# Row sums of the first tile on quarters of the PE array, and a fourth context slab held

## Chip, core and metric

The kernel runs on one core of one Trainium2 chip. The metric is device time in microseconds of that core. The engines are PE (TensorE, matrix products), DVE (VectorE), ACT (ScalarE), POOL (GpSimd) and SP (SyncE, which here only issues DMAs). PEld is the weight load of PE, which overlaps its matmuls.

## The reference

Two transformer blocks on 256 tokens of 1024 features, all in float32. The change touches the end of the first block (a mixture of single-neuron experts, "PEER") and the part of the second block that runs beside it (a feed-forward on a separate context of 256 tokens, and the same feed-forward on the 128 tokens of tile 0).

```python
def peer_ffn(h, ...):                # for each block of 128 tokens
    ... 8 heads x 16 chosen experts = 128 expert rows a token
    u_sel = peer_u[expert]
    a = gelu(einsum('bqhkd,bqd->bqhk', u_sel, hb))
    v_sel = peer_v[expert]
    return einsum('bqhk,bqhkd->bqd', g * a, v_sel)
x = x + gate2 * peer_ffn(...)
# second block, with x and with ctx
swiglu(h, w13, w2): a, b = split(h @ w13); (silu(a) * b) @ w2
```

## The kernel before

**Work around the change.** The 256 tokens are two tiles of 128. For each tile the kernel gathers 128 "slots": one indirect DMA by POOL (line 1387) brings, for each of the 128 tokens, the 2048 floats of one expert (u and v side by side), a row tile of 128x2048 float32. Eight buffers hold such row tiles (`GBUF = 8`). Two slots make a batch; tile 0 is batches 0 to 63 (the gather's first half), tile 1 is batches 64 to 127 (the second half).

**For every slot** DVE multiplies u by h and sums (line 2506, `dot_batch`), ACT turns the sum into a weight (lines 1900 and 1831), and then v is added with that weight. In tile 0, PE adds it: ACT makes a 128x128 diagonal matrix of the weights (line 1838), and `add_row` does eight matmuls, each with a 128x128 block of v as the stationary operand and the diagonal as the moving one; they accumulate over the 128 slots in two PSUM banks, features on partitions. In tile 1, DVE adds it instead (line 2517, `sum_batch`), but for the last two batches. A buffer is free for the next indirect DMA when PE (`row_free_pe`) or DVE (`row_free_dve`) has read it.

**Between the batches** PE works through a list of chunks (`context()`): first tile 1's queries and key scores, then the context's feed-forward. How many chunks are done by batch n is set by `context_due`: up to 29 batches one a batch, then evenly up to `CTX_FIRST` at batch 60, then `CTX_SECOND` more over tile 1. One 2 MB slab of w13 gives four chunks for the context (`ctx_hidden`, of which DVE and ACT drain the results) and two for tile 0 (`first_hidden`). Tile 0's can start only when its expert sum has been added to x (`expert_residual`) and normed (`first_norm`), so that the first slabs are held in the ring until then: `HELD = 3` slabs, of which `AHEAD = 2` have their context chunks in tile 0. The ring has four slots; slots 0 to 2 take context slabs in turn, slot 3 (`first_home`) is kept for tile 0's `h_first`, `hid_first` and `rstd_first`. SP loads a slab when the slot's last reader is through (line 1335). The slabs of what follows the gather wait for the last row tiles (line 1330).

## Time and profile before

| | |
|---|---|
| runs | 1710.43 us median of 3 (1707.39 to 1710.72) |
| span of the profiled execution | 1706.5 us (its whole time is not given apart; the span is 0.9 us under the lowest run and 3.9 us under the median) |
| PE, PEld busy | 1631.5 us, 1468.6 us |
| DVE, ACT, POOL busy | 1170.6, 661.6, 387.7 us |
| first and last indirect DMA of a row tile | 218.0 us, 993.2 us |
| moved by DMA | 538.50 MB, mean 316 GB/s |

Busy time is a sum over stages with different limits. The stage of the change is the gather, from 218 us to about 1000 us; how DMA, PE and DVE stand in it is to be read stretch by stretch. In the kernel's program a float32 matmul shows as two MATMUL records.

### The profile page before, as it was taken

What the parts mean: (1) busy time and instruction counts of PE and PEld (TensorE: products, weight loads), DVE (VectorE), ACT (ScalarE), POOL (GpSimd) and SP (SyncE); (2) the same over time, 40 slices, a digit from 0 to 9 for tenths busy, and PEclk for the clock granted to TensorE, in tenths of its full rate; (3) what the DMA queues carried; (4) which work ended last, traced back from release to release, by engine and by line L of the source; (5) the groups of instructions that cost most, each with busy time, mean ns of one, the idle gap of its engine ahead of it and who ended that gap; (6) DMA issues with size and microseconds to landing.
All of it is one profiled execution on the core that took longest, in us unless ns stands there. A gap on an engine that the chain in (4) does not pass through costs nothing.

```text
span 1706.5 us, 29058 instructions
## 1 busy us (share of the span) xinstructions
PE 1631.5 (96%) x11668; PEld 1468.6 (86%) x11668; DVE 1170.6 (69%) x1988; ACT 661.6 (39%) x1274; POOL 387.7 (23%) x317
## 2 busy tenths in 40 slices
PE   5999999998899899999997999999999999999997
PEld 3878889998799899998987557889998977989997
DVE  3675468777997678789887688564565457665554
ACT  3544233334333443433112148444444522444443
POOL 0463034434444434344443310000000000000000
PEclk9899999999999999999998999999999999999999
DMA  9768899999999999999999999865445522544442
GB/s 367 302 269 356 359 400 408 406 421 413 416 408 400 415 395 421 414 420 420 421 407 399 422 405 405 316 259 201 157 186 198 197 99 99 226 181 185 183 170 93
DMA packets 57732, 538.50 MB, mean 316 GB/s; under 512 B 6401, under 2 KB 6529, under 8 KB 7425
## 3 DMA queue, kind: packets, MB, share of 16 engines
q1 hardware_dynamic: 20592, 267.18, 39.6%
q0 software_dynamic: 37008, 269.50, 38.5%
q8 instruction: 92, 1.51, 0.4%
q14 instruction: 40, 0.32, 0.0%
HBM read 535.60 MB, written 1.05 MB: 314 GB/s over the span
## 4 chain that ended last, share of the span: by engine, by line
PE 64%; DMA 17%; DVE 9%; issue 6%; ACT 2%; POOL 1%; POOLq 0%; DVEq 0%; SPq 0%; ACTq 0%
PE psum L516 63%; DMA arena<-in_experts,idx_stage 15%; DVE arena L2517 4%; DVE arena L2506 1%; DMA ring<-in_w_ada 1%; DMA ring<-in_w_in 1%; POOL arena L1387 1%; DMA extra_float<-in_w_ada 1%; DVE ring_r L1996 0%; DVE arena L2628 0%; DVE small L2506 0%; POOL idx_stage L1380 0%; DVE arena_r L2062 0%; ACT h_t L1812 0%; DVE h_t L2209 0%
## 5 line engine op out<-in xcount | busy, mean ns | idle before, releaser
L2506 DVE CUSTOM_DVE_ANT_0 arena<-arena 128x1024 f32<-128x1024 f32 x256 | 313.9, 1226 | 134.0 <-DMA arena<-in_experts,idx_stage 127.9
L1387 POOL DMA_INDIRECT arena<-in_experts,idx_stage x256 | 302.4, 1181 | 367.8 <-DVE arena L2517 166.8
L1996 DVE TENSOR_TENSOR ring_r<-ring,ring_r 128x1024 fp32r<-128x1024 f32 (+1 forms) x200 | 240.8, 1214 | 196.1 <-ACT ring_r L1440 195.1
L516 PE MATMUL psum<-small_r,ring_r 128*128 128x256 f32 x1600 | 285.9, 283 | 3.4 <-DVE h_t_r L2077 3.4
L1440 ACT ACTIVATE ring_r<-ring 128x1024 fp32r<-128x1024 f32 (+1 forms) x200 | 208.3, 1048 | 169.5 <-PE psum L516 156.0
L516 PE MATMUL psum<-small,arena 128*128 128x128 f32 x2112 | 251.4, 279 | 19.9 <-ACT small L1838 19.9
L516 PEld LDWEIGHTS psum<-small,arena 128*128 128x128 f32 x2112 | 246.2, 196 | 23.6 <-ACT small L1838 21.0
L516 PE MATMUL psum<-h_t,ring 128*128 128x256 f32 (+1 forms) x1360 | 249.7, 342 | 3.0 <-DMA ring<-in_w_in 3.0
L516 PEld LDWEIGHTS psum<-small_r,ring_r 128*128 128x128 f32 x1600 | 245.0, 188 | 5.5 <-issue 5.2
L516 PEld LDWEIGHTS psum<-h_t,ring 128*128 128x128 f32 x1360 | 220.1, 192 | 24.5 <-DMA ring<-in_w_in 3.2
L516 PE MATMUL psum<-h_t_r,ring_r 128*128 128x256 f32 x800 | 223.6, 279 | 0.0
L516 PE MATMUL psum<-arena_r,ring_r 128*128 128x256 f32 x1488 | 209.6, 282 | 2.8 <-DVE arena_r L2062 2.8
L1900 ACT ACTIVATE small<-small 128x2 f32<-128x2 f32 x127 | 25.8, 203 | 462.6 <-DVE small L2506 462.6
L516 PEld LDWEIGHTS psum<-arena_r,ring_r 128*128 128x128 f32 x1488 | 190.8, 189 | 3.3 <-DVE arena_r L2062 3.3
L2517 DVE SCALAR_TENSOR_TENSOR arena<-arena,small 128x1024 f32<-128x1024 f32 x123 | 158.0, 1285 | 5.7 <-ACT small L1831 1.3
L516 PEld LDWEIGHTS psum<-h_t_r,ring_r 128*128 128x128 f32 x800 | 150.8, 189 | 0.1
L516 PE MATMUL psum<-arena,ring 128*128 128x128 f32 (+1 forms) x916 | 141.7, 315 | 0.0
L516 PEld LDWEIGHTS psum<-arena,ring 128*128 128x128 f32 x916 | 130.3, 191 | 10.7 <-issue 1.7
L516 PEld LDWEIGHTS psum<-ring 128*128 128x128 f32 x1056 | 121.8, 194 | 2.0 <-DVE ring L2457 1.1
L516 PE MATMUL psum<-ring 128*128 128x128 f32 x1056 | 121.9, 277 | 0.9 <-DVE ring L2457 0.9
L516 PE MATMUL psum<-ring_r,small_r 128*128 128x512 f32 x272 | 90.0, 398 | 0.7 <-DVE ring_r L1996 0.7
L516 PE MATMUL psum<-arena_r,upper 128*128 128x256 f32 x384 | 74.0, 295 | 9.8 <-DVE ring_r L1996 5.6
(279 smaller groups left out, 1704.8 us busy)
## 6 DMA issues: line engine op xcount, KB each, us to landing
ring<-in_w_in SPq DMA_DIRECT2D x31, 2048.0 KB, 8.4
ring<-in_w_ffn SPq DMA_DIRECT2D x29, 2048.0 KB, 11.2
ring<-in_w_ada SPq DMA_DIRECT2D x18, 2048.0 KB, 8.9
ring<-in_w_ffn SPq DMA_DIRECT2D x23, 1408.0 KB, 7.0
arena<-in_w_ada SPq DMA_DIRECT2D x8, 2048.0 KB, 15.6
ring<-in_w_out SPq DMA_DIRECT2D x4, 2048.0 KB, 9.2
ring<-in_peer_wq SPq DMA_DIRECT2D x4, 2048.0 KB, 10.2
extra_float<-in_w_ffn SPq DMA_DIRECT2D x4, 2048.0 KB, 12.8
```

Source lines behind the costliest of these rows:

```text
L516: return nc.tensor.matmul(o, a, b, start=first, stop=last)
L1387: nc.gpsimd.indirect_dma_start(rows[slot % GBUF], None, dram["experts"], bass.IndirectOffsetOnAxis(ap=idx_stage[:, slot:slot + 1], axis=0) ...
L1440: nc.scalar.activation(upper(i), whole(i, ring), ACT.Copy).then_inc(hi_made, 1)
L1900: nc.scalar.activation(acts[:, n % 8, :], dots[:, n % 8, :], ACT.Gelu_apprx_tanh).then_inc(sem("gelus"), 1)
L1996: nc.vector.tensor_tensor(whole(i, ring_r), whole(i, ring), upper(i).bitcast(F32), ALU.subtract).then_inc(lo_made, 1)
L2506: step(nc.vector.tensor_tensor_reduce(u, u, h2[:, n // PER_TILE, :], 1.0, 0.0, ALU.mult, ALU.add, dots[:, n % 8, s:s + 1]), sem("dots"))
L2517: ins = STT(y_sum, row, weight, y_sum, ALU.mult, ALU.add)
```

## The change

In tile 0 the row sum now uses that the weights are diagonal: only the 64x64 blocks on the diagonal hold something. `add_quarters` makes four matmuls for each slot in place of eight: the stationary operand is the 64x64 block of one half of the tokens, the moving one is v of those 64 tokens, 512 features wide. The two halves of the tokens use the upper and the lower 64 rows of the array and write to different banks; the two halves of the features use the left and the right 64 columns and write to different partitions. So a bank holds the 64 tokens of one half on its partitions, once for each half of the features, and features no longer stand on partitions: ACT copies them to SBUF (`copy_quarters`), PE turns them back with eight transposes (`turn_quarters`), and DVE adds them (`quarters_residual`). Since the four matmuls are in different quarters, each has a semaphore of its own (`row_read`), and POOL and ACT wait for all four where they waited for `row_free_pe`.

Slot 3 of the ring takes a fourth context slab (`HELD = 4`), and the context chunks of three slabs are in tile 0 (`AHEAD = 3`; `CTX_FIRST` goes from 42 to 46 chunks, `CTX_SECOND` from 112 to 108). `h_first` and `rstd_first` move elsewhere; `hid_first` still comes to slot 3, so slab 3 is read first (`HELD_ORDER`).

```diff
-HELD, AHEAD = 3, 2
+HELD, AHEAD = 4, 3
+HELD_ORDER = (3, 1, 2, 0)
...
-            slot = (n - ctx_at) % CTX_RING
+            slot = HELD - 1 if n == ctx_at + HELD - 1 else (n - ctx_at) % CTX_RING
...
+        row_read = [[sem(f"row_read_tokens{g}_features{j}") for j in range(2)] for g in range(2)]
+        quarters_copied = sem("quarters_copied")
...
+            def add_quarters(g):
+
+                row, weight = rows[g % GBUF], diag[:, g % (GBUF // 2), :]
+                for half in range(2):
+                    tokens = slice(64 * half, 64 * half + 64)
+                    for j in range(2):
+                        features = slice(D + BANK * j, D + BANK * j + BANK)
+                        mm(psum[64 * j:64 * j + 64, sum_banks[0][half], :], weight[tokens, tokens], row[tokens, features],
+                           g == 0, g == SLOTS - 1).then_inc(row_read[half][j], 1)
+
+            def turn_quarters():
+
+                for half in range(2):
+                    pe.wait_ge(quarters_copied, half + 1)
+                for i in range(2):
+                    o = begin(f"yt0_{i}", "dve")
+                    for c in (2 * i, 2 * i + 1):
+                        for half in range(2):
+                            at_c = c % 2 * L + half * P
+                            last = nc.tensor.transpose(o[:, at_c:at_c + P], y_quarters[:, half, c * P:(c + 1) * P], ident)
+                    ctx_end(f"yt0_{i}", last)
...
-                for i, w, n in held:
+                for i, w, n in (held[i] for i in HELD_ORDER):
                     yield from first_hidden(i, w)
                     release(n=n)
...
-                        ins = add_row(0, g, g, g == 0, g == SLOTS - 1)
-                        if g < SLOTS - 1:
-                            ins.then_inc(sem("row_free_pe"), 1)
+                        add_quarters(g)
...
+                if n == PER_TILE:
+                    turn_quarters()
...
-                if t == 0:
-                    pool.wait_ge(sem("row_free_pe"), r * ROUND + (known_round * ROUND + s + 1))
...
+                if t == 0 or known_round == 0 and s < GBUF:
+                    for read in itertools.chain(*row_read):
+                        pool.wait_ge(read, r * ROUND + (t * SLOTS + known_round * ROUND + s + 1))
...
+            def copy_quarters():
+
+                for half in range(2):
+                    for read in row_read[half]:
+                        act.wait_ge(read, GBUF + SLOTS)
+                    nc.scalar.activation(y_quarters[:, half, :], psum[:, sum_banks[0][half], :],
+                                         ACT.Copy).then_inc(quarters_copied, 1)
...
-                    expert_residual(0)
...
                 if n + 1 < BATCHES:
                     dot_batch(n + 1, range(1 if n + 2 == BATCHES else BATCH))
+                if n == PER_TILE:
+                    quarters_residual()
```

How the instructions stand. First PE, two of the early batches of tile 0, before; `small` is the diagonal, `arena` the row tile, `h_t,ring` a chunk of tile 1's query.

```order
L516 MATMUL psum<-small,arena 128x128 [waits diag]
L516 MATMUL psum<-small,arena 128x128 x7
L516 MATMUL psum<-h_t,ring 128x128 [waits act_drained,slab_landed1]
L516 MATMUL psum<-h_t,ring 128x128 x7
L516 MATMUL psum<-small,arena 128x128 [waits diag]
L516 MATMUL psum<-small,arena 128x128 x7
```

The same place now:

```order
L521 MATMUL psum<-arena,small 64x512 [waits diag]
L521 MATMUL psum<-arena,small 64x512 x3
L521 MATMUL psum<-h_t,ring 128x128 [waits act_drained,slab_landed1]
L521 MATMUL psum<-h_t,ring 128x128 x7
L521 MATMUL psum<-arena,small 64x512 [waits diag]
L521 MATMUL psum<-arena,small 64x512 x3
```

Four matmuls of 512 columns stand where eight of 128 columns stood; the chunk between them is as before. Then PE where tile 0 ends and tile 1 begins, before (`psum<-h_t,ring 128x256` is `ctx_hidden`, `psum<-ring 128x128` is `first_hidden`):

```order
L516 MATMUL psum<-small,arena 128x128 [waits diag]
L516 MATMUL psum<-small,arena 128x128 x7
L516 MATMUL psum<-h_t,ring 128x256 [waits act_drained,slab_landed2]
L516 MATMUL psum<-h_t,ring 128x256 x15
L516 MATMUL psum<-arena,ones 128x128 [waits dve_drained,sq_first]
```

and now:

```order
L521 MATMUL psum<-arena,small 64x512 [waits diag]
L521 MATMUL psum<-arena,small 64x512 x3
L521 MATMUL psum<-h_t,ring 128x256 [waits act_drained,slab_landed3]
L521 MATMUL psum<-h_t,ring 128x256 x7
L1008 MATMUL psum<-early,arena 128x128 [waits dve_drained,quarters_copied]
L1008 MATMUL psum<-early,arena 128x128 x3
L1008 MATMUL psum<-early,arena 128x128 [waits act_drained]
L1008 MATMUL psum<-early,arena 128x128 x3
```

The slab that tile 1 begins with is the fourth instead of the third, and the eight transposes have come in behind its first chunk. Last DVE at the same place, before (L2506 ISA is a dot, L2424 the addition of tile 0's expert sum to x, L2515 the first sum of tile 1):

```order
L2416 TENSOR_TENSOR small<-small 128x128 [waits dve_step]
L2424 SCALAR_TENSOR_TENSOR x_t<-psum,mod,x_t 128x128 [waits group_done,gates]
L2424 SCALAR_TENSOR_TENSOR x_t<-psum,mod,x_t 128x128 [waits dve_step] x3
L2424 SCALAR_TENSOR_TENSOR x_t<-psum,mod,x_t 128x128 [waits group_done,dve_drained]
...
L2506 ISA arena,small<-arena 128x1024 [waits row_landed2,dve_drained]
L2506 ISA arena,small<-arena 128x1024 [waits row_landed3,dots]
L2515 TENSOR_SCALAR arena<-arena,small 128x1024 [waits weights,dots]
```

and now:

```order
L2460 TENSOR_TENSOR small<-small 128x128 [waits dve_step]
L2563 ISA arena,small<-arena 128x1024 [waits row_landed2,gates]
L2563 ISA arena,small<-arena 128x1024 [waits row_landed3,dots]
L2470 SCALAR_TENSOR_TENSOR x_t<-psum,mod,x_t 128x128 [waits group_done,dots]
L2470 SCALAR_TENSOR_TENSOR x_t<-psum,mod,x_t 128x128 [waits dve_step] x3
L2470 SCALAR_TENSOR_TENSOR x_t<-psum,mod,x_t 128x128 [waits group_done,dve_drained]
...
L2572 TENSOR_SCALAR arena<-arena,small 128x1024 [waits weights,dve_drained]
```

The two dots have moved ahead of the additions to x.

## Rows read from the trace of the kernel before

**Rows 1.** Stretches of the gather: busy us of each engine, clock, DMA share, GB/s
```profile
core 0: us, PE busy (x) PEld busy (x) DVE busy (x) ACT busy (x) POOL busy (x), PEclk, DMA share, GB/s
218.00:285.00 67.00, 66.27 (x589) 61.71 (x588) 46.68 (x133) 26.32 (x77) 29.01 (x26) 1.00 1.00 414
285.00:315.00 30.00, 30.00 (x271) 30.00 (x271) 28.15 (x87) 10.11 (x30) 12.68 (x14) 1.00 1.00 385
360.00:425.00 65.00, 55.82 (x435) 53.95 (x434) 46.48 (x132) 21.80 (x66) 24.80 (x24) 0.89 1.01 420
425.00:480.00 55.00, 48.00 (x380) 46.21 (x379) 51.96 (x130) 20.09 (x63) 27.76 (x27) 0.97 1.00 404
480.00:530.00 50.00, 50.00 (x384) 48.17 (x383) 46.46 (x134) 15.82 (x53) 20.13 (x21) 1.00 1.01 419
530.00:545.00 15.00, 15.00 (x122) 14.59 (x121) 12.40 (x25) 6.68 (x19) 7.28 (x7) 1.00 0.94 362
595.00:620.00 25.00, 25.00 (x196) 24.17 (x196) 23.06 (x28) 15.10 (x31) 10.97 (x10) 1.00 0.94 368
620.00:880.00 260.00, 259.11 (x1569) 238.13 (x1569) 209.71 (x261) 79.23 (x172) 108.86 (x88) 1.00 1.01 420
880.00:920.00 40.00, 32.95 (x208) 30.34 (x206) 35.18 (x50) 12.32 (x32) 15.69 (x13) 0.91 0.97 381
218.00:1000.00 782.00, 748.39 (x5101) 680.62 (x5099) 625.81 (x1200) 254.08 (x691) 325.95 (x288) 0.98 1.00 412
```

**Rows 2.** Waits in tile 0's part, 216 to 620 us: total us, times, longest
```profile
POOL arena L1387 <- PE psum L516: 130.0, 72, 10.9
DVE arena L2506 <- DMA arena<-in_experts,idx_stage: 63.0, 46, 6.2
```

**Rows 3.** Waits in tile 1's part, 620 to 1001 us
```profile
POOL arena L1387 <- DVE arena L2517: 156.8, 42, 12.2
DVE arena L2506 <- DMA arena<-in_experts,idx_stage: 64.9, 33, 6.2
DVE x_t L2498 <- PE psum L516: 2.0, 1, 2.0
```

**Rows 4.** Waits of SP's own queue, whole span
```profile
SPq L1330 <- DMA arena<-in_experts,idx_stage: 34.4, 1, 34.4
```

**Rows 5.** Timeline of PE, 515 to 530 us: start, us, work
```profile
516.82 7.31 PE L516 MATMUL psum<-small,arena 128*128 128x128 f32 x64
523.96 3.62 PE L516 MATMUL psum<-h_t,ring 128*128 128x256 f32 x16
```

**Rows 6.** Timeline of PE, 57 to 66 us
```profile
58.21 4.55 PE L516 MATMUL psum<-arena 64*128 64x128 f32 x32
62.69 1.92 PE L516 MATMUL psum<-ring,silu 128*32 128x512 f32 x16
64.55 0.50 PE L516 MATMUL psum<-arena_r,upper 128*128 128x256 f32 x2
```

**Rows 7.** PE groups by form: count, busy us, mean ns
```profile
L516 PE MATMUL psum<-ring,silu 128*32 128x512 f32 x288 | 34.4, 597 | 1.2 <-ACT arena L1463 0.7 <-DMA ring<-in_w_ada 0.4
L516 PE MATMUL psum<-ring,h_t 128*128 128x512 f32 x128 | 55.4, 592 | 0.0
```

**Rows 8.** Timeline of all engines, 588 to 625 us
```profile
588.72 1.23 DVE L2506 CUSTOM_DVE_ANT_0 arena<-arena 128x1024 f32<-128x1024 f32 x1
589.99 1.23 DVE L2506 CUSTOM_DVE_ANT_0 arena<-arena 128x1024 f32<-128x1024 f32 x1
598.16 2.61 DVE L2517 SCALAR_TENSOR_TENSOR arena<-arena,small 128x1024 f32<-128x1024 f32 x2
600.25 1.32 POOL L1387 DMA_INDIRECT arena<-in_experts,idx_stage  x1 [4.83 <-DVE arena L2517]
609.18 14.62 SPq L1335 DMA_DIRECT2D ring<-in_w_ffn  x3
```

**Rows 9.** Timeline of ACT at a copy of a bank, 310 to 345 us
```profile
318.07 0.58 ACT L1463 ACTIVATE arena<-psum 128x512 f32<-128x512 f32 x1
```

**Rows 10.** DMA issues of two stretches (285 to 315, 545 to 590 us), median us to landing
```profile
arena<-in_experts,idx_stage POOLq DMA_INDIRECT x12, 8.1
arena<-in_experts,idx_stage POOLq DMA_INDIRECT x18, 11.6
```

More of the change, by code:

```diff
@@ L307, in program @@
         first_home = ring[:, SPLIT_RING * SLAB:(SPLIT_RING + 1) * SLAB]
-        h_first = first_home[:, 0:1024].rearrange("p (k t) -> p k t", k=KD)
-        hid_first = first_home[:, 1024:1024 + KF * P].rearrange("p (k t) -> p k t", k=KF)
-        rstd_first = first_home[:, 3840:3968]
+        h_first = arena[:, 4096:5120].rearrange("p (k t) -> p k t", k=KD)
+        hid_first = first_home[:, 0:KF * P].rearrange("p (k t) -> p k t", k=KF)
+        rstd_first = rstd[:, 0:P]
         sq_ctx = ([arena[:, 4096 + i * L:4096 + (i + 1) * L] for i in range(4)]
@@ L351, in program @@
         combo = arena[:, F0 + 5632:F0 + 6144].rearrange("p (h n) -> p h n", h=2)
+        y_quarters = arena[:, 4096:5120].rearrange("p (g n) -> p g n", g=2)
         pick = [arena[:, 4096:4096 + 2 * PSEL * PSEL], small[:, 1536:1536 + 2 * PSEL * PSEL]]
@@ L1081, in context @@
                     for n, _ in enumerate(ctx_hidden(i, w)):
-                        if i == AHEAD and n == 1:
+                        if i == AHEAD and n == 2:
                             pe.wait_ge(sem("sq_first"), 1)
@@ L1188, in _ @@
                         pe.wait_ge(sem("diag"), g + 1)
-                        ins = add_row(0, g, g, g == 0, g == SLOTS - 1)
-                        if g < SLOTS - 1:
-                            ins.then_inc(sem("row_free_pe"), 1)
+                        add_quarters(g)
                 if n == PER_TILE - 1:
+                    for half in range(2):
+                        tenant[sum_banks[0][half]] = (quarters_copied, half + 1)
                     cycle[:] = range(BANKS)
+                if n == PER_TILE:
+                    turn_quarters()
             assert next(ctx_chunks, "none") == "none" and taken_chunks == CTX_FIRST + CTX_SECOND, taken_chunks
@@ L1364, in row_open @@
             def row_open(t, known_round, r, s):
-                if t == 0:
-                    pool.wait_ge(sem("row_free_pe"), r * ROUND + (known_round * ROUND + s + 1))
-                elif known_round == 0 and s < GBUF - 1:
-                    pool.wait_ge(sem("row_free_pe"), SLOTS + s + 1)
-                elif known_round == 0 and s == GBUF - 1:
-                    pool.wait_ge(group_done, index["yt0_1"] + 1)
+                if t == 0 or known_round == 0 and s < GBUF:
+                    for read in itertools.chain(*row_read):
+                        pool.wait_ge(read, r * ROUND + (t * SLOTS + known_round * ROUND + s + 1))
                 else:
@@ L1721, in _, with rows_credit @@
             mod_steps(16, 17, False)
+            def rows_credit():
+                for read in itertools.chain(*row_read):
+                    act.sem_inc(read, GBUF // 2)
+            def copy_quarters():
+                for half in range(2):
+                    for read in row_read[half]:
+                        act.wait_ge(read, GBUF + SLOTS)
+                    nc.scalar.activation(y_quarters[:, half, :], psum[:, sum_banks[0][half], :],
+                                         ACT.Copy).then_inc(quarters_copied, 1)
             def copy_query(t, i):
@@ L1739, in _ @@
             mod_steps(17, 19, False)
-            act.sem_inc(sem("row_free_pe"), GBUF // 2)
+            rows_credit()
             def context_norm(tag, shift):
@@ L1781, in first_hidden @@
                 def first_hidden(i):
-                    yield done_at[f"fx_a{i}"] + 1
+                    yield done_at[f"fx_{'b' if i == HELD - 1 else 'a'}{i}"] + 1
+                    if i == HELD - 1:
+                        act.wait_ge(group_done, index[f"fx_b{i}"] + 1)
                     drain(nc.scalar.activation(flat(hid_first[:, 2 * i:2 * i + 2, :]), take(f"fx_a{i}")[:, 0:L], ACT.Silu))
@@ L1798, in context @@
                                          scale=scale_of["x1"][:, k:k + 1]).then_inc(sem("h_first"), 1)
-                for i in range(HELD):
+                for i in HELD_ORDER:
                     yield from first_hidden(i)
@@ L1836, in diagonal @@
                 act.wait_ge(sem("weights"), g + 1)
-                act.wait_ge(sem("row_free_pe"), GBUF + min(turn - GBUF // 2 + 1, SLOTS - 1))
+                for read in itertools.chain(*row_read):
+                    act.wait_ge(read, GBUF + min(turn - GBUF // 2 + 1, SLOTS))
                 nc.scalar.activation(diag[:, turn % (GBUF // 2), :], ident, ACT.Identity,
@@ L1903, in _ @@
                     due = next(ctx_steps, None)
+                if n == PER_TILE - 1:
+                    copy_quarters()
             for _ in ctx_steps:
@@ L2416, in gates, with quarters_residual @@
                 step(TT(bt, bt, total.unsqueeze(2).to_broadcast([P, hs.stop - hs.start, PSEL]), ALU.mult), sem("gates"))
+            def quarters_residual():
+                for i in range(2):
+                    o = take(f"yt0_{i}").rearrange("p (c g j t) -> p c g j t", c=2, g=2, j=2)
+                    for c in range(2):
+                        for j in range(2):
+                            k = 4 * j + 2 * i + c
+                            xs = x_t[:, k, 0:P].rearrange("p (g t) -> p g t", g=2)
+                            ins = STT(xs, o[:, c, :, j, :], mod1[:, 40 + k:41 + k], xs, ALU.mult, ALU.add)
+                            if c + j < 2:
+                                step(ins)
+                    drain(ins)
             def expert_residual(t):
@@ L2463, in context @@
                     yield from ctx_hidden(i)
-                for i in range(HELD):
+                for i in HELD_ORDER:
                     yield from first_hidden(i)
```

2 lines of the change are left out of this document (1 added, 1 removed).

## The prediction, made before the changed kernel ran

> **What bounds the kernel now.** I read the busy time by stretch first. From 218 us to the end of the gather the DMA column is at 1.00 or 1.01 and moves 420 GB/s wherever nothing is short: 260 us on end in tile 1, and most of tile 0 [rows 1]. PE is busy nearly all of the same time, so the busy column alone doesn't say who sets the pace. The waits do. In tile 0 DVE waits 63.0 us for row tiles to land, and in tile 1 another 64.9 us, while it waits for a PE result only 2.0 us in tile 1 [rows 2, 3]. So the transfers set the pace of both halves; PE keeps up and no more. The work behind the gather hangs on it too: SP stands 34.4 us at line 1330, until the last row tiles have landed, before it loads the slabs of what follows [rows 4]. What the change is worth is therefore the time by which the last row tile lands earlier, and that is bytes over 420 GB/s plus the time in which the transfers fall short of it. The bytes don't change.
>
> The reader is to see in [rows 1] where they fall short, and how much full-speed time is lost there, us x (420 - GB/s) / 420: 285 to 315 us, 30 x 35/420 = 2.5; 425 to 480 us, 55 x 16/420 = 2.1; 530 to 545 us, 15 x 58/420 = 2.1; 595 to 620 us, 25 x 52/420 = 3.1; 880 to 920 us, 40 x 39/420 = 3.7; the start, 67 x 6/420 = 1.0. Together 14.5 us of 782. This is all that any speeding up of PE can win here while the gather stays one of transfers.
>
> **The row sums.** A batch of two slots is 16 matmuls, 32 records, before: 64 records take from 516.82 to the next start at 523.96, 7.14 us, so 3.57 us a batch and 0.112 us a record [rows 5]. After it is 8 matmuls, 16 records of 512 columns. Such a record alone takes 55.4/128 = 0.433 us; the records with 32 stationary columns, which use four column groups in turn, take 34.4/288 = 0.119 us [rows 7]: four run at once. A burst of 16 of them goes from 62.69 to the next start at 64.55, 1.86 us [rows 6]. For 64 rows the trace has only a burst of 32 records in which the upper and lower half of the array alternate: the view merges two widths in it, 4.55 us, 0.142 us a record. No row shows rows and columns halved together. Bounds for a batch: 1.86 us if four quarters run at once, 16 x 0.433 = 6.9 us if none do. I take 1.9 us, since the burst of four column groups is the nearest row with the same 512 columns. PE then has 64 x (3.57 - 1.9) = 107 us less to do in tile 0.
>
> The Trainium skill, TensorEngine Tiling (Array Packing), Tiling Modes, says that changing the tiling mode drains the engine; here that happens twice a batch. The burst above holds both changes: 16 records at 0.433/4 us are 1.73 us, so some 0.13 us of its 1.86 us are left for them, and the sum does not move. The Trainium skill, TensorE: Matmul & The Clock Gate, The cost: per-tile semaphore tail, gives about 26 ns for each semaphore increment that a matmul makes on completion; six more a batch would be an estimated 0.16 us, 10 us of PE in tile 0, which no row here shows apart. Both speak against the change and both are small beside 107 us.
>
> **What that opens.** Between the batches PE does a chunk of 3.62 us at 523.96 [rows 5], from batch 29 on 13 such chunks over 31 batches before and 17 after. PE's need per batch there is 3.57 + 13/31 x 3.6 = 5.1 us before, against 2 x 1.049 MB / 420 GB/s = 5.0 us for two row tiles: PE is just late, which is why POOL waits 130.0 us for it in 72 places [rows 2]. After it is 1.9 + 17/31 x 3.6 = 3.9 us. Buffers come free sooner, and more row tiles are in flight. That this matters for the rate is seen at 285 to 315 us: a row tile lands 8.1 us after its issue, some three in flight, at 385 GB/s, against 11.6 us later [rows 10, 1]. I count the dips of tile 0 as won where PE is the one waited for: 2.5 and 2.1 whole (285 and 530 us), and half of the 2.1 at 425 us, since DVE is busy 51.96 of 55 us there. That is 5.6 us, say 5.7 with a little of the start.
>
> **The fourth slab.** It moves one load of 2 MB, 2.1/420 = 5.0 us of transfer, from tile 1 to tile 0, right behind the two at the end of the queries. Where transfers set the pace of both halves this is nothing in the sum: tile 0 is 5.0 us longer and tile 1 5.0 us shorter. The cover is DVE's 64.9 us of waiting in tile 1; if it were gone, the slab would cost 5.0 us. Four chunks (14.5 us of PE) go the same way, under the room just made. SP's first load in tile 1 stood at 609.18 [rows 8]; it comes after four chunks of `first_hidden` now, not two, so the transfers run for about 8 us longer on row tiles alone, at the pace of DVE. That pace is two dots and two sums, 588.72 to 589.99 is 1.27 for a dot and 2.61 for two sums, so about 2 x 1.27 + 2.61 = 5.2 us for two row tiles against 5.0 [rows 8]: 8 x 4% = 0.3 us.
>
> **The change of tiles.** Here a wait is added. DVE must have tile 0's sum before its first sum of tile 1, and behind it stand all sums, and behind these POOL's next indirect DMA. New on the way: two copies by ACT at 0.58 us [rows 9], the rest of a context chunk of up to 3.62 us that stands before the transposes, and 16 records of transposes at 0.112 us, 1.8 us. Together 3 us at least and 6.6 us at most. On the other side two dots, 2.5 us, have moved ahead of the wait. Net 0.5 to 4.1 us later on DVE. Before, DVE was busy 23.06 of 25 us here and POOL waited 4.83 us for it [rows 8, 1], so little hides it; but PE is no longer late with the last batches, which gives back some. Bounds -1 and 4.1; I take 0.5.
>
> POOL waits for four semaphores where it waited for one, ACT as well. POOL is busy 325.95 of the gather's 782 us, at most 29.01 of 67 in a stretch [rows 1], so extra instructions of a few tenths of a microsecond a row tile lie under its waits.
>
> **The sum**, against the profiled span of 1706.5: -5.7 +0.3 +0.5 = -4.9, so 1701.6. The median of the runs is 3.9 above that span, so the forecast is 1705.5 us.
>
> **The rivals.**
> Nothing to be measured: DVE, not PE, makes the dips. For it: DVE 28.15 of 30 us at 285 and 23.06 of 25 at 595 us. Against: POOL's 130.0 us on PE in tile 0. Recovery would be 1.6 and the wait at the change of tiles 4.1: 1713. With half the recovery, 1708.5; or the forecast's gain with the slab's 5.0 us not given back, 1710.5. These are one outcome, 1708 to 1713. Chance 0.30.
> Larger gain: with PE early everywhere, the dips at 595 and 880 us go too, 6.8 us more, 1699. For it: at 880 us PE runs out of work and its clock is 0.91 [rows 1]. Against: both are stretches on row tiles alone, where DVE's 5.2 us rule. Chance 0.12.
> Slower: the quarters don't run four at once. At two at once a batch is 16 x 0.433/2 = 3.5 us, PE's need from batch 29 on is 3.5 + 2.0 = 5.5 us against 5.0, 31 x 0.5 = 15 us late where it was 3 late before, so +12, of which the slab's 5.0 can come back in tile 1: 1717. At none at once it is 6.9 us a batch, +64 x 3.3 = 211 us. It decides against the change from about 0.17 us a record on. Against: column groups do run four at once in the burst. Chance 0.08.
> The forecast: chance 0.50.
>
> **How the numbers follow.** A measurement of this kernel can tell 0.2%, 3.4 us, from no change. Of the forecast's 0.50 I put 0.43 beyond that and 0.07 within; the larger gain adds 0.12 to faster; of the middle case 0.20 is within and 0.10 above. So faster 0.55, same 0.27, slower 0.18. The range reaches from the larger gain with some of its room, 1697, to the middle case's upper end and the lower end of two at once, 1716.
>
> **What would show it.** The records psum<-arena,small of 64x512 should number 1024 and take 0.11 to 0.12 us each; POOL's wait for PE in tile 0 should fall from 130 us to under 50, and DVE's for landings rise. The 285 us and 530 us dips should be gone and the last indirect DMA be issued near 988 us in place of 993.2. A third w13 load should follow the two near 357 us. The prediction is wrong if the records take over 0.17 us, if the rate between 600 and 625 us falls well under 368, or if the row tiles come as late as before while PE is idle: then DVE or ACT was the one to wait for.

## The result, and the profile after

The changed kernel takes 1718.48 us (median of 4 runs, 1717.25 to 1718.73) against 1710.58 us (median of 4, 1707.39 to 1715.04): a ratio of 1.0045, 95% interval 1.0028 to 1.0061. It is slower by 7.7 us. The forecast was 5 us less than before, 1705.5 us, with a range of 1697 to 1716 us, and the measured time lies outside it. The profiled execution has a span of 1716.9 us and took 1718.73.

Busy time by stretch in the changed kernel (columns as in [rows 1]):

```profile
core 0: us, PE busy (x) PEld busy (x) DVE busy (x) ACT busy (x) POOL busy (x), PEclk, DMA share, GB/s
...
285.00:315.00 30.00, 23.76 (x200) 14.85 (x193) 28.14 (x84) 10.75 (x34) 14.14 (x14) 1.00 1.02 421
395.00:420.00 25.00, 9.05 (x56) 3.24 (x56) 19.06 (x63) 8.76 (x30) 8.33 (x8) 0.70 1.01 420
420.00:440.00 20.00, 13.78 (x80) 7.18 (x80) 14.26 (x31) 7.04 (x14) 7.72 (x8) 0.82 0.72 278
440.00:480.00 40.00, 31.14 (x176) 13.86 (x176) 37.78 (x96) 17.12 (x51) 19.16 (x19) 0.83 1.01 420
...
530.00:545.00 15.00, 9.74 (x54) 5.02 (x53) 14.14 (x37) 3.80 (x15) 6.29 (x7) 0.89 1.01 419
...
595.00:610.00 15.00, 13.43 (x74) 11.74 (x73) 9.58 (x18) 6.42 (x9) 2.20 (x3) 1.00 0.88 346
610.00:640.00 30.00, 25.58 (x213) 25.58 (x214) 29.13 (x35) 14.23 (x35) 14.06 (x11) 0.89 0.84 319
...
880.00:920.00 40.00, 33.33 (x171) 29.85 (x170) 35.06 (x46) 7.15 (x22) 17.80 (x16) 0.91 1.01 410
```

The reader is to see three things against [rows 1]. The dips at 285 and 530 us are gone (421 and 419 GB/s for 385 and 362), and the one at 880 us is nearly gone (410 for 381). A new hole is at 420 us: 278 GB/s over 20 us, 20 x 142/420 = 6.8 us of transfer time. And the change of tiles has grown from 3.1 us to 15 x 74/420 + 30 x 101/420 = 9.9 us. The ledger against before: from 420 to 480 us 6.8 less the 2.1 lost there before, 4.7 lost; at the change of tiles 9.9 less 3.1, 6.8 lost; at the three dips 2.5 + 2.1 + 2.7 won. That is 4.2 us net. The gather, from the first indirect DMA to SP's first load behind the last row tiles, says the same: 782.3 us before (217.99 to 1000.25), 786.2 after (220.16 to 1006.36).

Waits in tile 0's part, 216 to 630 us: total us, times, longest.

```profile
POOL arena L1413 <- PE psum L521: 139.3, 51, 16.7
PE psum L521 <- ACT small L1880: 83.6, 35, 7.9
DVE arena L2563 <- DMA arena<-in_experts,idx_stage: 70.2, 54, 6.2
```

Before, PE waited 18.5 us for ACT's weights in this part; now it waits 83.6 us.

The row sums by form: 1024 records, as they should be.

```profile
L521 PE MATMUL psum<-arena,small 64*64 64x512 f32 x1024 | 143.8, 687 | 83.8 <-ACT small L1880 83.6
```

That is 0.140 us a record, with both clocks in it. Timeline of PE at two batches of 16 records:

```profile
398.57 3.69 PE L521 MATMUL psum<-arena,small 64*64 64x512 f32 x16 [7.87 <-ACT small L1880]
403.73 1.95 PE L521 MATMUL psum<-arena,small 64*64 64x512 f32 x16
```

All four quarters run at once: 1.95 us, as forecast. But PE now stands idle for much of the time, and its granted clock is lower (0.70 of full speed from 395 to 420 us, so part of it at 1.2 GHz; 0.87 there before). Right behind other work of PE (the second row) a batch takes 1.95 us, but behind a gap of 7.87 us the same batch takes 3.69, what a batch on the whole array took at 2.4 GHz (3.57). The clock granted within the two rows is 0.50 in the first (1.2 GHz) and 1.00 in the second (2.4 GHz). The Trainium skill, TensorE: Matmul & The Clock Gate, What's actually happening, says that the clock is halved after PE has been idle; the two rows agree.

Timeline at the hole of 420 us (start, us, work, idle before it and what ended it):

```profile
411.92 1.26 POOL L1413 DMA_INDIRECT arena<-in_experts,idx_stage  x1 [0.30 <-issue]
...
418.82 0.68 ACT L1880 ACTIVATE small<-early,small 128x128 f32<-128x128 f32 x2
419.40 1.90 ACT L1492 ACTIVATE arena<-arena 128x2048 f32<-128x2048 f32 x1
...
421.35 6.52 PE L521 MATMUL psum<-arena,ones 128*128 128x256 f32 x16 [10.84 <-ACT arena L1492]
...
427.80 5.38 PE L521 MATMUL psum<-arena,small 64*64 64x512 f32 x48
...
429.92 0.94 POOL L1413 DMA_INDIRECT arena<-in_experts,idx_stage  x1 [16.74 <-PE psum L521]
```

PE waits 10.84 us for ACT's squares of the context (L1492), then sums them for 6.52 us, and the row sums of three batches stand behind it (48 records). POOL gets no buffer for 16.74 us and the transfers run dry. Timeline at the change of tiles:

```profile
595.24 1.04 PE L1008 MATMUL psum<-early,arena 128*128 128x128 f32 x8
596.12 7.07 PE L521 MATMUL psum<-h_t,ring 128*128 128x256 f32 x32
...
599.84 1.51 DVE L2470 SCALAR_TENSOR_TENSOR x_t<-psum,mod,x_t 128x128 f32<-128x128 f32 x4 [1.38 <-PE psum L521]
...
603.03 1.95 PE L521 MATMUL psum<-arena,ones 128*128 128x128 f32 x16
...
604.81 3.62 PE L521 MATMUL psum<-h_t,ring 128*128 128x256 f32 x16
...
608.47 0.37 ACT L1833 ACTIVATE rstd<-psum,small 128x128 f32<-128x128 f32 x1 [2.81 <-PE psum L521]
...
613.27 1.32 POOL L1413 DMA_INDIRECT arena<-in_experts,idx_stage  x1 [7.72 <-DVE arena L2574]
...
630.79 7.47 SPq L1364 DMA_DIRECT2D ring<-in_w_ffn  x2
```

Twice a result is there and its reader goes on one chunk later. The transposes end at 596.3, DVE reads the second half at 599.84. The sum of squares of tile 0 ends at 605.0, ACT reads it at 608.47, when the chunk behind it ends. Not all of the two times 3.5 us is lost: DVE was at the first half until 598.47 and stood idle 1.38 us, ACT loaded a table until 605.65 and stood idle 2.81 us. The code says why: PE has one semaphore for all results (`group_done`), a reader waits for "as many results as were begun up to mine", and both now stand inside a chunk that is begun and not ended. For the transposes that is their place behind the chunk at batch 64. For the squares it is one line of the change that the diff ahead of the prediction left out, and that also puts them one part of a chunk later:

```diff
-                        if i == AHEAD and n == 1:
+                        if i == AHEAD and n == 2:
```

Last, the timeline behind the gather:

```profile
1007.17 5.44 PE L521 MATMUL psum<-small,arena 128*128 128x128 f32 x32 [3.93 <-ACT small L1880]
...
1017.18 3.05 DVE L2481 SCALAR_TENSOR_TENSOR x_t<-psum,mod,x_t 128x128 f32<-128x128 f32 x8 [5.96 <-PE psum L521]
...
1018.83 3.67 PE L521 MATMUL psum<-ring,h_t 128*128 128x512 f32 x8 [0.87 <-DVE x_t L2481]
```

and the same three before:

```profile
1001.05 3.81 PE L516 MATMUL psum<-small,arena 128*128 128x128 f32 x32 [1.32 <-ACT small L1838]
...
1009.43 3.06 DVE L2424 SCALAR_TENSOR_TENSOR x_t<-psum,mod,x_t 128x128 f32<-128x128 f32 x8 [4.33 <-PE psum L516]
...
1010.06 3.60 PE L516 MATMUL psum<-ring,h_t 128*128 128x512 f32 x8
```

Tile 1's first row sums take 5.44 us for 3.81, behind 3.93 us without work (granted clock 0.69 within them, 1.00 before), and PE's chunk behind DVE's addition starts 1.65 us after DVE's start, not 0.63. SP's loads that hang on these are 8.73 and 8.66 us apart before, and 10.45 and 9.76 after.

### The profile page after: what moved, and what is told of

Same layout as the page of the kernel before. It is cut to its first block, busy times and chain, and to the rows that moved or that the text cites. A ratio compares the mean times of both kernels' runs of the same rounds, so it can differ in the third digit from the quotient of the medians.

```text
span 1716.9 us, 27352 instructions
## 1 busy us (share of the span) xinstructions
PE 1555.5 (91%) x10652; PEld 1281.9 (75%) x10652; DVE 1167.3 (68%) x1988; ACT 660.0 (38%) x1274; POOL 386.0 (22%) x317
## 3 DMA queue, kind: packets, MB, share of 16 engines
q8 instruction: 84, 1.38, 0.3%
## 4 chain that ended last, share of the span: by engine, by line
PE 53%; DMA 23%; DVE 12%; issue 8%; ACT 3%; POOL 1%; POOLq 0%; DVEq 0%; SPq 0%; ACTq 0%
PE psum L521 52%; DMA arena<-in_experts,idx_stage 21%; DVE arena L2574 4%; DVE arena L2563 2%; POOL arena L1413 1%; DMA ring<-in_w_ada 1%; DMA ring<-in_w_in 1%; DMA extra_float<-in_w_ada 1%; DVE ring_r L2040 0%; POOL idx_stage L1406 0%; DVE small L2563 0%; DVE arena L2686 0%; ACT small L1880 0%; DVE arena L2378 0%; DVE small L2376 0%
## 5 line engine op out<-in xcount | busy, mean ns | idle before, releaser
L1413 POOL DMA_INDIRECT arena<-in_experts,idx_stage x256 | 297.2, 1161 | 369.7 <-DVE arena L2574 157.5
L521 PE MATMUL psum<-h_t,ring 128*128 128x256 f32 (+1 forms) x1360 | 253.3, 344 | 0.0
L521 PE MATMUL psum<-arena,ring 128*128 128x128 f32 (+1 forms) x1620 | 224.5, 300 | 10.3 <-ACT arena L1837 6.0
L521 PE MATMUL psum<-arena,small 64*64 64x512 f32 (+1 forms) x1056 | 157.9, 684 | 83.8 <-ACT small L1880 83.6
L521 PEld LDWEIGHTS psum<-arena,ring 128*128 128x128 f32 x1620 | 212.2, 193 | 22.2 <-ACT arena L1837 6.4
L521 PEld LDWEIGHTS psum<-arena,small 64*64 64x64 f32 (+1 forms) x1056 | 42.8, 148 | 165.3 <-ACT small L1880 124.0
L1388 POOL TENSOR_TENSOR ring_r<-ring,upper 128x1024 fp32r<-128x1024 f32 x24 | 62.6, 2628 | 92.4 <-ACT upper L1466 92.4
L521 PEld LDWEIGHTS psum<-arena_r,upper 128*128 128x128 f32 x384 | 63.7, 204 | 14.0 <-DVE ring_r L2040 5.6
```

What stands on the lines that cost most here:

```text
L521: return nc.tensor.matmul(o, a, b, start=first, stop=last)
L1388: nc.gpsimd.tensor_tensor(whole(i, ring_r), whole(i, ring), upper(i).bitcast(F32), ALU.subtract).then_inc(lo_made, 1)
L1413: nc.gpsimd.indirect_dma_start(rows[slot % GBUF], None, dram["experts"], bass.IndirectOffsetOnAxis(ap=idx_stage[:, slot:slot + 1], axis=0) ...
```

## The experiments

All ratios are to the kernel before. "Gather" is its length in the profiled execution, as above.

| run | what differs | ratio (95%) | gather, us |
|---|---|---|---|
| (before) | | 1 | 782.3 |
| (after) | | 1.0045 (1.0028 to 1.0061) | 786.2 |
| turn_first | after, transposes ahead of the chunk | 1.0039 (1.0027 to 1.0052) | 786.8 |
| order_both | turn_first, and squares of tile 0 one part earlier, outside a chunk's halves | 1.0014 (1.0005 to 1.0023) | 782.3 |
| ctx_later | after, context's chunk and ACT's squares 2 batches later | 1.0061 (1.0048 to 1.0074) | 792.8 |
| all_three | order_both and ctx_later | 1.0033 (1.0021 to 1.0044) | 786.8 |
| ctx_free | after, the chunk behind ACT's squares | 1.0031 (1.0021 to 1.0041) | 784.6 |
| order_and_ctx | order_both and ctx_free | 1.0002 (0.9990 to 1.0013) | 781.4 |
| quarters_only | after, with three slabs and the squares where they were before | 0.9982 (0.9972 to 0.9993) | 779.0 |
| slab_only | before, with four slabs (old row sums) | 1.0075 (1.0060 to 1.0090) | 791.6 |
| quarters_bank | quarters_only, own banks for the transposes | 0.9976 (0.9962 to 0.9990) | 779.0 |
| quarters_bank_turn | quarters_bank, transposes first | 0.9977 (0.9965 to 0.9989) | 779.6 |
| quarters_best | quarters_bank_turn, ctx_free's order | 0.9961 (0.9946 to 0.9977) | 779.7 |
| quarters_best2 | the same kernel again | 0.9975 (0.9963 to 0.9987) | 776.8 |
| tail_busy | order_both, chunks of tile 1 one batch longer | 1.0008 (0.9993 to 1.0024) | 783.3 |
| slab_all_fixed | four slabs, all repairs of this list | 0.9999 (0.9988 to 1.0010) | 783.2 |

**turn_first and order_both.**

```diff
+                if n == PER_TILE:
+                    turn_quarters()
                 while taken_chunks < context_due(n):
...
-                if n == PER_TILE:
-                    turn_quarters()
```

order_both also takes `n == 2` back to `n == 1`.

> The changed kernel, with the eight transposes of tile 0's expert sum ahead of the context chunk at batch 64 in place of behind it. In the changed kernel the chunk's result is open at that point (two of its four parts done), and PE's results are counted in the order in which they are begun: the second four transposes end at 596.3 us and DVE goes on at 599.8. Theory 'late signal': transposes start some 2 us earlier and their second half is read at once, so DVE's additions end at about 598.5 in place of 601.4; POOL's wait of 8.2 us there falls to 5 or 6, and the time falls by 2 to 3 us, to a ratio of 1.003. Rival 'DVE is the bound after the change of tiles' (9.7 of 10 us busy from 610 to 640): the DVE work that is queued is the same, the ratio stays at 1.0045.

> As the run with the transposes first, and the sum of squares of tile 0 (the one ahead of the norm) behind the second part of the fourth slab's chunks, where no result is open, in place of behind the third. In the changed kernel it ends at 605.0 us and ACT reads it at 608.5. Theory 'late signal': ACT reads it within 0.3 us of its end, h_first is ready about 5 us earlier than in the changed kernel, POOL's second wait of 7.7 us falls under 5, SP's first load in tile 1 comes near 625 in place of 630.8, the stretch from 595 to 640 us loses some 4 us of transfer time in place of 9.9, and the ratio is 1.001. Rival 'DVE is the bound': the ratio stays at 1.0045, and SP's load comes earlier without a gain.

turn_first won 0.06%, which its interval doesn't tell from nothing (0.15% was expected); order_both won 0.25% on top, 4.3 us. The squares and their reader in turn_first:

```profile
600.97 1.95 PE L521 MATMUL psum<-arena,ones 128*128 128x128 f32 x16
...
606.41 0.37 ACT L1833 ACTIVATE rstd<-psum,small 128x128 f32<-128x128 f32 x1 [4.45 <-PE psum L521]
```

Timeline of order_both:

```profile
593.16 3.05 DVE L2470 SCALAR_TENSOR_TENSOR x_t<-psum,mod,x_t 128x128 f32<-128x128 f32 x8
...
597.36 2.05 PE L521 MATMUL psum<-arena,ones 128*128 128x128 f32 x16 [0.74 <-ACT arena L1831]
...
600.53 0.37 ACT L1833 ACTIVATE rstd<-psum,small 128x128 f32<-128x128 f32 x1
...
605.34 1.32 POOL L1413 DMA_INDIRECT arena<-in_experts,idx_stage  x1 [4.92 <-DVE arena L2574]
...
621.08 0.33 SPq L1364 DMA_DIRECT2D ring<-in_w_ffn  x1
```

DVE adds the two halves in one piece, ACT no longer waits for a chunk, and POOL's wait is 4.92 us, for 9.35 in turn_first and 7.72 in the changed kernel. SP's first load stands at 621.08 for 630.79; 3.1 us of that is the gather's earlier start (217.04 for 220.16). So the place of the squares is shown as a cause, 4.3 us, and the rival (DVE rules there anyway) falls. But the edit does two things. From DVE's first addition (594.61 in turn_first, 593.16 here) to ACT's read of the sum are 11.80 us in turn_first and 7.37 here. Of the 4.4 us between them 2.2 come because the squares no longer stand behind a further part of the chunk (they start 6.36 and 4.20 us after that addition), and 2.4 because ACT reads their sum 1.12 us after its end and not 3.49. The late signal is thus about half of it by the rows; no run parts the two.

**ctx_later, all_three and ctx_free.** The first moves `CTX_START` to 31. ctx_free has

```diff
-CTX_START = 29
+CTX_START = 32
...
-                yield CTX_START + 2
+                yield CTX_START - 1
                 act.wait_ge(sem("ctx_landed"), 16)
```

> The changed kernel, with the chunk that sums the context's squares taken at batch 31 in place of 29 (CTX_START 31). Theory 'the context is waited for': PE came to this chunk 5.8 us after the gather of the context was issued and waited 10.8 us for it, with the row sums behind it, and POOL waited 16.7 us. Two batches later, 10 us, the context has landed: both waits go, the rate from 420 to 440 us is 420 in place of 278 GB/s, and 4 to 6.5 us are won: a ratio of 1.001 to 1.002. Rival 'the row sums are late for another reason' (DVE's selection of experts stands at the same place): POOL's longest wait stays over 10 us and the ratio at 1.0045.

> The three edits of this call together: transposes first, the sum of squares where no result is open, the context's chunk at batch 31. If the three losses are separate, their gains add up: 5 to 10 us under the changed kernel, a ratio of 0.998 to 1.001 and a gather that ends near 997 us in place of 1006. If DVE's own work is what limits the gather after the change of tiles, only the part in tile 0 counts and it is 1.001 to 1.002, or it is given back by later waits and nothing is won.

My first theory of the hole at 420 us, that PE waits for the context's transfer, fell: ctx_later is slower still. Its timeline:

```profile
430.68 1.89 ACT L1492 ACTIVATE arena<-arena 128x2048 f32<-128x2048 f32 x1
...
432.63 5.97 PE L521 MATMUL psum<-arena,ones 128*128 128x256 f32 x16 [12.00 <-ACT arena L1492]
...
440.00 0.19 POOL L1406 COPY idx_stage<-ids 128x8 uint32 x1 [16.59 <-PE psum L521]
```

The wait is as long as in the changed kernel, 11 us later. all_three, expected at 1.001 or under, came to 1.0033, 3.2 us above order_both: the later place of the pair costs there too. ACT squares at batch `CTX_START + 2`, behind the weights of that batch, and PE takes its chunk at `CTX_START`, ahead of the row sums: PE waits for two batches of DVE and ACT, wherever the pair stands. Before, the same order cost 4.0 us of waiting on PE.

> The changed kernel, with PE's chunk that sums the context's squares at batch 32 and ACT's squaring behind the weights of batch 31. In the changed kernel PE takes the chunk ahead of the row sums of batch 29 and ACT squares only behind the weights of batch 31, so PE waits for two batches that DVE and ACT still have to do; the run with both moved two batches later kept that distance, and its wait (12.0 us on PE, 16.6 us on POOL) stood there as before. Theory 'order between the engines': with the distance turned round PE's wait falls under 1 us, POOL's longest wait in tile 0 under 9 us, no stretch between 400 and 480 us runs under 400 GB/s, and 4 to 6 us are won: a ratio of 1.001 to 1.002. Rival 'the context's transfer is what is waited for': ACT then waits for it at batch 31, and the weights behind it are late; POOL's wait stays over 12 us and the ratio at 1.0045.

> The edit of the run before in this call, and the two of the run that moved the transposes and the sum of squares out of open results (1.0014). If the two places are separate, the gains add up: 4 to 6 us under 1.0014, a ratio of 0.998 to 0.999, and a version that beats both kernels. If DVE's own pace in the second half limits the gather, what is won in tile 0 is lost later: 1.001.

ctx_free against the changed kernel: 0.14%, 2.4 us; on order_both 0.12%, 2.0 us, where 4 to 6 us were expected of each. Neither gain is clear of the intervals; the gathers are 1.6 and 0.9 us shorter. No wait for L1492 is left in tile 0's part. Stretches of ctx_free:

```profile
420.00:440.00 20.00, 13.80 (x80) 5.42 (x72) 16.50 (x35) 5.37 (x16) 7.98 (x8) 0.83 1.01 420
440.00:480.00 40.00, 24.18 (x120) 9.88 (x121) 38.55 (x105) 17.08 (x52) 14.78 (x15) 0.74 0.93 377
```

The hole is gone, and 40 x 43/420 = 4.1 us come back right behind it, where DVE is busy 38.55 of 40 us: it has the norm of the context and the choice of experts side by side there. So 6.8 us became 4.1: the order between the engines made the hole, and mending it wins less than the hole was worth.

**quarters_only and slab_only.** The two halves of the change apart: `HELD, AHEAD = 3, 2` with `HELD_ORDER = (0, 1, 2)` and `n == 1`; and the kernel before with the slab's part of the diff, `n == 1`.

> The row sums on quarters alone: three slabs held, two of them multiplied in tile 0, as before the change (and the sum of squares of tile 0 behind the second part, as before). Theory 'the losses come with the quarters' (PE is early and waits at the context's chunk; the transposes are signalled late) and the slab costs little: 1.001 to 1.002, PE's wait for the context's squares still near 10 us. Rival 'the slab's 5.0 us in tile 0 are not given back': a ratio of 0.997 to 0.999, under before.

> The fourth slab alone, with the row sums on the whole array as before, and the sum of squares behind the second part. PE has 17 chunks in place of 13 over 31 batches at 3.57 us of row sums a batch: 5.5 us a batch against 5.0 of transfer, so PE is late by up to 12 us in tile 0 and 5.0 us come back in tile 1. Theory 'the slab needs the faster row sums': 1.002 to 1.005, POOL's wait for PE in tile 0 over 130 us. Rival 'PE's lateness is covered by the transfers of the slab': 1.000.

Both expectations missed: quarters_only came out at its rival's 0.997 to 0.999, and slab_only above the 1.002 to 1.005 of its theory. The quarters alone win 0.18%, 3.1 us; with the slab added it is +0.45%, so the slab's part, with `n == 2`, costs 0.63%, 10.8 us. On the old row sums, with `n == 1`, it costs 0.75%, 12.8 us. On quarters with `n == 1` (order_both against quarters_only) it costs 0.32%, 5.5 us: the slab does need the faster row sums. Stretches of quarters_only:

```profile
420.00:440.00 20.00, 12.38 (x86) 3.76 (x84) 18.05 (x43) 6.84 (x19) 9.69 (x9) 0.83 0.93 367
...
595.00:610.00 15.00, 14.83 (x107) 13.78 (x106) 14.49 (x18) 10.70 (x24) 4.63 (x5) 1.00 0.86 329
610.00:640.00 30.00, 30.00 (x212) 28.35 (x211) 19.16 (x25) 10.45 (x18) 12.10 (x9) 1.00 1.00 415
```

With three slabs the hole at 420 us is 2.5 us, not 6.8, and 610 to 640 us run at 415 GB/s, since SP's first load of tile 1 comes at 608.6. The change of tiles loses 3.3 + 0.4 = 3.6 us here, against 3.1 before: with the transposes, but without the slab, it costs 0.5 us. The last indirect DMA goes out at 989.6.

**quarters_bank, quarters_bank_turn, quarters_best.** The first has one edit:

```diff
-                    o = begin(f"yt0_{i}", "dve")
+                    o = begin(f"yt0_{i}", "dve", bank=sum_banks[0][i])
```

> The row sums on quarters alone (0.9982), with the two transposed halves written to the two banks that held the row sums, in place of the next two of the rotation. In the runs with quarters the addition of tile 1's sum goes to the next slab load in 9.8 us (1006.66 to 1016.42), in those without in 8.7 (1010.25 to 1018.91): PE waits there for DVE to read a bank. Theory 'two more results taken from the rotation move every later one by two banks': the 9.8 us become 8.7, and the rest of the kernel is as before; 1.1 us, a ratio of 0.9975. Rival 'it is PE's clock or something else of the quarters': 9.8 us and 0.9982 stay.

> As the run before in this call, with the transposes ahead of the chunk at batch 64. In the changed kernel this edit alone won 1 us. Theory 'late signal': the second half is read at once, DVE's additions to x end some 2 to 3 us earlier, and the rate from 595 to 610 us rises from 329: a ratio of 0.996 to 0.997. Rival 'PE stands idle until ACT's copies are there, and DVE waits for row tiles anyway': 0.9975 as without it.

> As the run before in this call, with PE's chunk for the context's squares at batch 32 and ACT's squaring behind the weights of batch 31. With four slabs held this won 2 us (1.0014 to 1.0002, 1.0045 to 1.0031). With three PE waits 4.1 us for ACT there in place of 10.8, and the stretch from 420 to 440 us runs at 367 GB/s. If the order between the engines matters with three as well, POOL's longest wait falls from 10.4 us to under 9 and 1 to 2 us are won: 0.995 to 0.996. If DVE's norm of the context, which now comes beside the selection of experts, takes it back, the ratio is that of the run before.

PE's first chunk behind tile 1's sum, in quarters_only:

```profile
1007.50 3.67 PE L521 MATMUL psum<-ring,h_t 128*128 128x512 f32 x8 [0.87 <-DVE x_t L2481]
```

and in quarters_bank:

```profile
1005.59 3.60 PE L521 MATMUL psum<-ring,h_t 128*128 128x512 f32 x8
```

The step to SP's next load is 9.76 or 9.77 us in all nine profiles with quarters and rotated banks (the changed kernel among them) and 8.65 to 8.67 in the seven others. Two results more in the rotation, and 400 us later a chunk gets a bank that DVE is still reading: 1.1 us, shown by the profiles; the times (0.9982, 0.9976) can't tell it. The transposes first won nothing here (0.9977), as the rival had it. quarters_best came to 0.9961, just above its 0.995 to 0.996, and once more, as quarters_best2, to 0.9975, just above the 0.9950 to 0.9972 expected of it.

**tail_busy.** `CTX_LAST = PER_TILE - 2` on order_both.

> Four slabs held, the transposes and the sum of squares out of open results (1.0014), and the last chunks of tile 1 spread to batch 125 in place of 124. With four slabs held PE has no work for 3.9 us ahead of the first row sum of the last batches, and these 32 records take 5.44 us, against 3.81 us with 1.3 us idle before them. Theory 'PE's granted clock falls in the gap that the four chunks moved to tile 0 leave': with work up to the row sums they take 3.8 us, and the time from the loads at line 1364 to tile 1's sum is 9.6 us in place of 11.3. Rival 'the row sums are late, not slow': it stays at 11.3 or grows by the chunk in front, 1 to 3 us.

```profile
1002.24 3.81 PE L521 MATMUL psum<-small,arena 128*128 128x128 f32 x32 [0.21 <-ACT small L1880]
```

With PE busy up to the row sums they take 3.81 us, where order_both has 6.45 (granted clock 1.00 for 0.57), and the first of the two steps 8.69 us for 11.48. The gap that the four moved chunks leave, 3.4 to 4.4 us of idle PE in seven profiles (slab_only, with the old row sums, among them), goes with row sums of 5.44 to 6.45 us, 1.6 us at least above 3.81. It is not so every time: in ctx_later they take 3.81 us at a clock of 1.00 behind 3.13 us of idle. Nor does the whole time show the gain: 1.0008 for 1.0014 is within the intervals, and the gather was 1 us longer.

**slab_all_fixed and quarters_best2**, on one chip.

> Four slabs held, with every repair found so far: transposes and the sum of squares of tile 0 out of open results, the context's chunk at batch 32 with ACT's squaring at 31, the transposes' results in the banks of the row sums, the chunks of tile 1 spread to batch 125. Theory 'the slab has a cost of its own': the row sums on quarters with three slabs have 0.9961; this comes to 1.0002 less 1.1 us (banks) and 1.6 us (row sums at the lower clock), 0.9986, some 4 us above three slabs, because SP's first load of tile 1 still comes near 621 us and the transfers between 595 and 640 us and between 440 and 480 us still fall short by 8 us together. Rival 'the slab costs only what its side effects cost' (the prediction's own reckoning, where what tile 0 loses tile 1 gives back): 0.996 to 0.997, as three slabs.

> The version with three slabs, all other repairs but the last, once more, on the same chip as the run with four: 0.9961 before, expected within 0.9950 to 0.9972.

0.9999 against 0.9975: with every side effect repaired that was found, the slab still costs 0.24%, 4.1 us, as the theory of a cost of its own had it (0.9986 was expected, and it came out 2 us higher). Against order_and_ctx (1.0002) the last two repairs won 0.5 us, not the 2.7 reckoned: the two steps behind the gather are 2.1 us shorter, but the gather is 1.9 us longer. The stretches of slab_all_fixed

```profile
440.00:480.00 40.00, 27.34 (x125) 11.41 (x126) 38.55 (x106) 17.66 (x50) 13.49 (x15) 0.70 0.91 358
...
595.00:610.00 15.00, 13.75 (x80) 11.91 (x79) 14.31 (x22) 10.23 (x20) 4.48 (x5) 1.00 0.88 336
610.00:640.00 30.00, 30.00 (x256) 29.59 (x256) 25.36 (x31) 15.01 (x26) 14.05 (x11) 1.00 0.99 400
```

and of quarters_best2

```profile
440.00:480.00 40.00, 23.94 (x136) 7.93 (x140) 38.79 (x97) 17.05 (x51) 17.88 (x16) 0.83 1.01 412
...
595.00:610.00 15.00, 14.83 (x110) 13.86 (x109) 14.61 (x16) 10.51 (x22) 5.04 (x5) 1.00 0.90 343
610.00:640.00 30.00, 30.00 (x211) 28.35 (x210) 18.02 (x24) 9.84 (x17) 11.10 (x9) 1.00 1.00 416
```

The largest difference lies in the stretch from 440 to 480 us, 5.9 us against 0.8. The other profiles with this order of the context say the same less sharply: 3.6 and 4.1 us with four slabs (order_and_ctx, ctx_free), 1.3 with three (quarters_best). quarters_best and quarters_best2 are one kernel, and their gathers differ by 2.9 us, so a single profile is no better than that. DVE is busy nearly throughout in all five, with 15 dots in these 40 us with four slabs, and 16 and 17 with three. Why DVE keeps the transfers fed with three slabs there and not with four is not settled; the slab's 5.0 us of transfer move all row tiles behind it later against the batches at which the choice of experts and the context's norm stand, but no run took that apart.

## Why the prediction was wrong

**What bounds the kernel** was right as far as it went: the transfers set the pace, and the time followed their shortfalls. Gather and ratio go together through the runs, but for the steps behind the gather and some microseconds from profile to profile.

**The row sums** were right where the clock is full: 1.95 us a batch against 1.9, and the rival "not four at once" falls. From one batch's start to the next chunk's are 1.88 us (301.14 to 303.02), 0.02 more than in the burst that the forecast went by: the 0.16 us estimated for six more increments don't show. Over all of tile 0, with both clocks, a record took 0.140 us and not 0.11 to 0.12, and PE's row sums fell from 243.8 to 143.8 us of busy time, by 100 us where 107 were forecast.

**What that opens** is half right. The dips of 285 and 530 us are gone as counted. The half dip at 425 us was not won. The reading behind it failed: "PE is just late, which is why POOL waits 130.0 us for it". With 100 us less of row sums for PE, POOL waits 139.3 us for it, where under 50 was forecast; in all sixteen profiles, with three slabs or four, it is 119.8 to 147.8 us (126.9 in quarters_only). The wait goes in a circle: POOL for a buffer that PE reads, PE for ACT's weights (83.6 us), ACT for DVE's dots, DVE for row tiles to land (70.2). With eight buffers and transfers that set the pace POOL waits for whoever reads last; so I read it, no run tests it. The last indirect DMA came at 999.3, not near 988, but at 989.6 with the quarters alone. The quarters' part was forecast at -5.7 + 0.5 = -5.2 us; alone, with three slabs, they measure -3.1 (-4.8 to -1.2), with -1.1 to come from the banks. So the quarters' part had its sign, and its size lies just outside that interval.

**The fourth slab** is the step that failed: "where transfers set the pace of both halves this is nothing in the sum", +0.3 us. It measures 10.8 us with what came with it. Two parts of that are measured by times: 4.3 for the place of the squares of tile 0 (order_both against turn_first), and 4.1 that stay when all that was found is repaired (slab_all_fixed against quarters_best2). Two more are weaker: about 2 of the context's order (2.4 and 2.0 us were won by ctx_free's edit with four slabs; with three the two runs of it, 0.9961 and 0.9975, against 0.9977 don't say more than 0 to 2.7), and 1.6 for the row sums at the lower clock, by profiles alone. Together they are 12.0; they overlap within their intervals of 2 to 3 us. The reckoning "tile 0 is 5.0 us longer and tile 1 5.0 us shorter" holds for the bytes. It may have left out that every wait at a fixed batch now meets row tiles 5 us later, which no run shows; the mechanism of the last 4.1 us stays open. That the chunks fit "under the room just made" was right in part: the slab costs 12.8 us on the old row sums and 5.5 on quarters with the squares in the same place. I had also placed the third load wrongly: it came at 381.7 us, not at 357.

**The change of tiles**: the bounds of -1 to 4.1 us counted copies, transposes and the rest of a chunk, each for its time. They did not count when the result is signalled. DVE went on 3.5 us after the transposes' end (1.38 of it idle), ACT 3.5 us after the squares' (2.81 idle). The stretch from 595 to 640 us lost 6.8 us more than before, above the upper bound. With the quarters alone it lost 0.5 us more, the number taken, so the rest came with the slab and `n == 2`. That 0.5 was met is in part luck: the transposes were counted too high (8 records and 1.04 us, not 16 and 1.8), and the late signal at them, 1.5 us of idle DVE in quarters_only, was not counted. Among the rivals the one with 4.1 us here and 1713 us in the end named this place, though not the size; "slower" with 1717 us is nearer to 1718.48 by number only, for the quarters do run four at once.

**Waits for four semaphores** on POOL and ACT were costed at nothing. No run took them apart; the quarters' gain leaves room for little.

**Behind the gather** I looked for nothing. Two steps are there: 1.1 us by the banks, and 1.6 by the clock, which one four-slab profile (ctx_later) doesn't have.

**Chances.** Slower had 0.18, all of it for the middle case and for quarters that don't overlap. A mechanism for the slab to cost more than its 5.0 us was not among the rivals, though the edit `n == 1` to `n == 2` stood in the whole diff.

## What to carry to other kernels

When an edit takes work off an engine, look for the waits that its lateness had hidden: places where its program stands ahead of another engine's at a fixed step. The chain of semaphores is to be read in the code too: with one counter for all results, a result that is begun inside another is seen only when the outer one ends. A wait in a ring of buffers names who reads last, not who is slow. And test the parts of a change apart, each alone and both together: here one half won 0.2% and the other lost 0.6%, and that other half costs more without the first; the quarters with three slabs and the two orders mended are at 0.996 to 0.998 of the kernel before.

## What was unexpected of the hardware

A batch of row sums on quarters took 1.95 us behind PE work and 3.69 us behind 7.9 us of idle; 32 records of 128 columns took 3.81 us behind 1.3 us of idle (and behind 3.13 in ctx_later) and 5.44 us behind 3.9. A PE with less to do was slower in the very bursts that others wait for. From SP's load behind tile 1's sum (1018.91 us before, 1027.76 after) to the end, where all kernels do the same, the profiled executions differ by up to 4.9 us (687.2 to 692.1), which is why single profiles are read here by stretch and not by span.
